# A hybrid decoder layer on one core: the third group's chain moved beside the next head pair's first inverse

## What is computed

```python
def step(S, inp):
    r_t, w_t, k_t, v_t, kk_t, b_t = inp
    sa = jnp.einsum('bhvk,bhk->bhv', S, -kk_t)
    S = S * w_t[:, :, None, :] + sa[..., None] * b_t[:, :, None, :] + v_t[..., None] * k_t[:, :, None, :]
    y = jnp.einsum('bhvk,bhk->bhv', S, r_t)
    return S, y
_, ys = lax.scan(step, S0, (tm(r), tm(decay), tm(k), tm(v), tm(kk), tm(b)))
# per head: y = (y - mean) * rsqrt(var + GN_EPS) * gn_w + gn_b, then
bonus = jnp.sum(r * k * r_k, axis=-1, keepdims=True) * v
y = y + bonus
```

## Time and profile before

| | us |
|---|---|
| median of 3 runs (1468.05 to 1469.26) | 1469.11 |
| profiled execution, device time | 1467.6 |
| its span | 1465.8 |
| TensorE matmul busy (PE) | 1352.2 |
| VectorE busy (DVE) | 722.3 |
| ScalarE busy (ACT) | 663.2 |
| GpSimd busy (POOL) | 475.7 |
| chain that ended last: TensorE 73%, VectorE 18%, ScalarE 5% | |

### The profile page before, as it was taken

One profiled execution on the slowest core, in us unless ns is written; L12 is line 12 of the kernel. 1 busy time (PEld: TensorE's weight loads), 2 busy tenths in 40 slices (PEclk: granted clock), 3 DMA queues, 4 the chain that ended last, 5 costly groups with the idle time before them and its releaser, 6 DMA issues.

```text
span 1465.8 us, 23803 instructions
## 1 busy us (share of the span) xinstructions
PE 1352.2 (92%) x9393; PEld 1141.8 (78%) x9393; DVE 722.3 (49%) x1562; ACT 663.2 (45%) x1518; POOL 475.7 (32%) x362
## 2 busy tenths in 40 slices
PE   4998989999899898998999998999999999989997
PEld 3987778777787777877768786888888888668885
DVE  5236574675755767557665543444434444540013
ACT  4334545555455454554545463444444434432221
POOL 2341222322322222232222232343433343334443
PEclk9999999999999999999999999999999999999998
DMA  5231111111111111111111121222222222225433
GB/s 200 75 88 44 44 46 52 48 41 52 46 44 53 44 44 53 44 47 44 50 44 46 56 74 51 79 73 73 73 80 70 75 73 72 72 64 171 150 97 136
DMA packets 151263, 102.23 MB, mean 70 GB/s; under 512 B 6398, under 2 KB 140640, under 8 KB 149600
## 3 DMA queue, kind: packets, MB, share of 16 engines
q1 hardware_dynamic: 151152, 100.71, 23.1%
HBM read 96.49 MB, written 4.19 MB: 69 GB/s over the span
## 4 chain that ended last, share of the span: by engine, by line
PE 73%; DVE 18%; ACT 5%; issue 2%; POOL 1%; DMA 0%; DVEq 0%; ACTq 0%; SPq 0%
PE tile L518 41%; DVE arena L1408 2%; PE tile L784 2%; DVE arena L1385 2%; PE tile L786 2%; PE tile L785 2%; PE ma L750 2%; PE ma L638 2%; DVE arena L1342 2%; PE ma L662 1%; DVE arena L1397 1%; DVE arena L1337 1%; PE mb L765 1%; PE mb L710 1%; PE mb L705 1%
## 5 line engine op out<-in xcount | busy, mean ns | idle before, releaser
L1125 POOL TENSOR_TENSOR w_lo<-w_raw,w_hi 128x512 fp32r<-128x512 f32 x324 | 426.6, 1317 | 940.8 <-ACT w_hi L854 940.6
L518 PE MATMUL tile<-hn_hi,w_hi 128*128 128x264 f32 (+1 forms) x1696 | 452.2, 329 | 0.0
L518 PE MATMUL tile<-hn_lo,w_hi 128*128 128x264 f32 (+1 forms) x1696 | 434.0, 319 | 0.0
L518 PE MATMUL tile<-hn_hi,w_lo 128*128 128x264 f32 (+1 forms) x1696 | 431.6, 318 | 0.3
L854 ACT CAST w_hi<-w_raw 128x512 fp32r<-128x512 f32 x324 | 200.5, 619 | 315.1 <-PE tile L518 205.8
L518 PEld LDWEIGHTS tile<-hn_hi,w_hi 128*128 128x128 f32 x1696 | 277.5, 190 | 32.9 <-issue 16.1
L518 PEld LDWEIGHTS tile<-hn_hi,w_lo 128*128 128x128 f32 x1696 | 275.8, 189 | 15.7 <-ACT arena L1013 1.7
L518 PEld LDWEIGHTS tile<-hn_lo,w_hi 128*128 128x128 f32 x1696 | 275.6, 189 | 13.5 <-issue 0.5
L1413 DVE TENSOR_TENSOR arena<-ma,c 128x384 f16<-128x384 f32 x120 | 66.6, 555 | 84.3 <-PE ma L638 84.1
L1010 ACT ACTIVATE arena<-ma 128x384 f16<-128x384 f32 x120 | 58.6, 488 | 46.4 <-PE ma L655 43.6
L1013 ACT ACTIVATE arena<-ma 128x384 f16<-128x384 f32 x120 | 58.2, 485 | 0.0
(11 more groups left out here) (248 smaller groups left out, 2145.4 us busy)
## 6 DMA issues: line engine op xcount, KB each, us to landing
w_raw<-w_in SPq DMA_DIRECT2D x260, 256.0 KB, 2.8
w_raw<-w_out SPq DMA_DIRECT2D x64, 256.0 KB, 3.0
big<-x SPq DMA_DIRECT2D x4, 1024.0 KB, 8.1
arena<-x SPq DMA_DIRECT2D x4, 1024.0 KB, 9.5
out<-big SPq DMA_DIRECT2D x3, 1024.0 KB, 3.9
arena<-post_norm_w SPq DMA_DIRECT2D x1, 1024.0 KB, 4.9
out<-big SPq DMA_DIRECT2D x2, 512.0 KB, 3.2
arena<-table_rope SPq DMA_DIRECT2D x2, 264.0 KB, 2.9
```

What stands on the lines that cost most here:

```text
L518: last = mm(o[:, at:at + n], w[:, slot, cols], t[:, kt, tok:tok + n], start=(kt == 0 and w is w_hi and t is hn_hi), stop=(kt == KT - 1 and ...
L1125: T(w_lo[:, slot, :], w_raw[:, slot, :], w_hi[:, slot, :].bitcast(F32), ALU.subtract).then_inc(s("lo_done"), 1)
```

## The change

- The late chain of group 2 no longer lies in the next pair's stage but beside its first inverse: `chain_at` puts a chain's step at step 4.25 + n of the inverse of group (g+1) mod 3, right behind an inverse step. In iteration 9 (attention) it stays at the start.
- For that, what the late chain still reads gets a place of its own: a second set of suv for the last three chunks (`chunk_home`), a second `w_end`, and a third `bk_tok` and `b_in`; `wu` and `au` share their columns, `tha` its place with `lv`.
- The first inverse starts at place 11.5 instead of 12.5, an inverse takes 17.2 slots instead of 16.8. The bonus goes from place 24 to 12.8, the group norm from 10.68 to 25.2.
- `ar_pads` of groups 1 and 2 are two pieces; the last one comes at the end of the first inverse.
- The level masks are made one per level, each behind the sum before it, and the two k masks at levels 2 and 3, where both stood together at the start.

No arithmetic changes. The core of the diff:

```diff
-        INV_AT, INV_SPAN, INV_STEPS = 12.5, 16.8, 15.19
-        CHAIN_LAG, CHAIN_SPAN, CHAIN_STEPS = 0.18, 16, 11
-        LATE_AT, LATE_SPAN = 4.97, 7.71
-        GN_AT = 10.68
-        BONUS_AT = 24
-        GATE_AT = 24
+        INV_AT, INV_SPAN, INV_STEPS = 11.5, 17.2, 15.19
+        CHAIN_FROM = 4.25
+        LATE_AT, LATE_STEP = 0.85, 0.7
+        GN_AT = 25.2
+        BONUS_AT, BONUS_DVE = 12.8, 15.3
+        GATE_AT = 37.5
-        REST_DVE = (8.58, 9.5, 13.5)
+        REST_DVE = (8.58, 9.3, 10, 10.6)
-        LEVEL_1, LEVEL_2 = 1.6, 3.92
+        LEVEL_1 = 1.6
+        MASK_AFTER = (2, 3)
...
-        def chain_at(g, step, late, work="rwkv"):
-            if late:
-                return (LATE_AT if work == "rwkv" else 0.5) + LATE_SPAN * step / CHAIN_STEPS
-            return INV_AT + INV_SPAN * (g + 1) + CHAIN_LAG + CHAIN_SPAN * step / CHAIN_STEPS
+        def chain_at(g, step, late, work):
+            if late and work == "attn":
+                return LATE_AT + LATE_STEP * step
+            return inv_at((g + 1) % NG, CHAIN_FROM + step)
+
+        def chunk_home(i, ch, late=0):
+
+            return ch + GC * ((i - late) % 2) if ch >= NC - GC else ch
...
-                    yield chain_at(g, 0.5 + 3 * c, late, work)
+                    yield chain_at(g, 3 * c, late, work)
...
-                yield chain_at(NG - 1, 3 * GC - 1, True)
-                if gn:
-                    dve.wait_ge(s("u_done"), n * NC - NC)
-                ar_pads(rest)
                 yield REST_DVE[2]
                 STT(rkp[:, 0:TP], xr[:], column(par, PC["r_k"], i - 1), kp, ALU.mult,
                     ALU.mult).then_inc(s("rkp_made"), 1)
-                yield BONUS_AT + 0.5
+                yield REST_DVE[3]
+                ar_pads(middle)
+                yield BONUS_DVE
                 dve.wait_ge(s("bonus_done"), n)
                 TT(mixed(i - 1), mb[:, 0:SEQ], xv[:, CH:TP], ALU.mult).then_inc(s("bonus_taken"), 1)
-                yield chain_at(0, 0, 0) - 0.5
+                yield inv_at(0, 12.8)
+                if gn:
+                    dve.wait_ge(s("u_done"), (n - 1) * NC)
+                ar_pads(last_)
...
                 for l in range(1, LEVELS):
                     yield inv_at(g, 1.7 + 2 * l)
                     dve.wait_ge(s("zz_done"), n * 5 + (l - 5))
                     TT(g3(z16), g3(ma[:, 0:W]), every(ident16), ALU.add).then_inc(s("zz_taken"), 1)
-                    if l == 1:
-                        yield inv_at(g, LEVEL_2)
-                        for l2 in range(2, LEVELS):
-                            level(l2, l4[:, l2 - 1])
-                        TT(g3(ab_lo), ab32, g3(ab_hi), ALU.subtract).then_inc(s("levels_made"), 1)
+                    yield inv_at(g, 1.8 + 2 * l)
+                    if l + 1 < LEVELS:
+                        level(l + 1, l4[:, l]).then_inc(s("level_made"), 1)
+                    else:
+                        TT(g3(ab_lo), ab32, g3(ab_hi), ALU.subtract).then_inc(s("lo_kept"), 1)
+                    if l in MASK_AFTER:
+                        yield inv_at(g, 2.6 + 2 * l)
+                        dve.wait_ge(s("kb_copied"), n)
+                        mask_k(MASK_AFTER.index(l))
```

More of the change, by code:

```diff
@@ L161, in hybrid_layer @@
         t512b = tanh_g[:]
-        ARENA = 16184
+        ARENA = 16192
         arena = sb("arena", [P, ARENA])
@@ L179, in hybrid_layer @@
         gn_pow = carve("rwkv", "gn_pow", 8)
-        wu = carve("rwkv", "wu", P)
-        au = carve("rwkv", "au", P)
+        wu = au = carve("rwkv", "wu_au", P)
         ew = carve("rwkv", "ew", NC * (CH + 1))
         ew3 = ew.rearrange("p (c t) -> p c t", c=NC)
-        w_end = carve("rwkv", "w_end", NC)
+        w_ends = [carve("rwkv", f"w_end{b}", NC) for b in range(2)]
         kk_small = carve("rwkv", "kk_small", 2 * TG)
@@ L192, in hybrid_layer, with several @@
         bk = carve("rwkv", "bk", NC * P).rearrange("p (c t) -> p c t", c=NC)
[L193 to L200, removed]
+        suv = carve("rwkv", "suv", (NC + GC) * P).rearrange("p (c t) -> p c t", c=NC + GC)
+        def several(count, name, n, dt=F32):
+            return [carve("rwkv", f"{name}{b}", n, dt) for b in range(count)]
+        bk_tok = several(NG, "bk_tok", GC * P)
+        t_t = several(2, "t_t", GC * P)
+        b_in = several(NG, "b_in", GC * 2 * P)
         b_in3 = [v.rearrange("p (c t) -> p c t", c=GC) for v in b_in]
@@ L208, in hybrid_layer @@
         emi = carve("rwkv", "emi", TPX)
-        tha = carve("rwkv", "tha", TP)
         kk = carve("rwkv", "kk", TP)
         kp = carve("rwkv", "kp", TP)
+        shared = taken["rwkv"]
+        tha = carve("rwkv", "tha", TP)
+        taken["rwkv"] = shared
+        lv = carve("rwkv", "lv", (LEVELS - 1) * GC * P, F16)
         ab_hi = carve("rwkv", "ab_hi", GC * P, F16)
         ab_lo = carve("rwkv", "ab_lo", GC * P, F16)
-        lv = carve("rwkv", "lv", (LEVELS - 1) * GC * P, F16)
         x16 = carve("rwkv", "x16", GC * P, F16)
@@ L1018, in chain_act @@
                     ch = g * GC + c
-                    yield chain_at(g, 0.8 + 3 * c, late, work)
+                    home = suv[:, chunk_home(i, ch, late), :]
+                    yield chain_at(g, 3 * c + 0.3, late, work)
                     if 0 < ch < SC:
@@ L1022, in chain_act @@
                         if ch == 1:
-                            act.wait_ge(s("ends_made"), i)
+                            act.wait_ge(s("ends_made"), i - late)
                         for h, rows in enumerate(halves):
-                            last = A(state0[rows, :], suv[rows, ch, rows], ACT.Copy, scale=w_end[rows, ch:ch + 1])
+                            last = A(state0[rows, :], home[rows, rows], ACT.Copy, scale=w_end_of(i, late)[rows, ch:ch + 1])
                         last.then_inc(s("s_scaled"), 1)
-                    yield chain_at(g, 1.8 + 3 * c, late, work)
+                    yield chain_at(g, 3 * c + 1.3, late, work)
                     if 0 < ch < SC:
@@ L1030, in chain_act @@
                     act.wait_ge(s("u_done"), chunks_so_far(i, ch, late))
-                    A(suv[bottom, ch, bottom], mb[bottom, bottom], ACT.Copy).then_inc(s("u_lower_taken"), 1)
-                yield chain_at(g, 9, late, work)
+                    A(home[bottom, bottom], mb[bottom, bottom], ACT.Copy).then_inc(s("u_lower_taken"), 1)
+                yield chain_at(g, 8.4, late, work)
                 act.wait_ge(s("y_done"), n)
@@ L1399, in inv_dve, with mask_k @@
                 yield inv_at(g, LEVEL_1)
-                level(1, l4[:, 0]).then_inc(s("level_1_made"), 1)
-                yield inv_at(g, 2)
-                dve.wait_ge(s("kb_copied"), n)
+                level(1, l4[:, 0]).then_inc(s("level_made"), 1)
                 cs = slice(g * GC, (g + 1) * GC)
-                for h, rows in enumerate(halves):
+                def mask_k(h):
                     other = halves[1 - h]
```

88 lines of the change are left out of this document (47 added, 41 removed).

## The result

| | before | changed |
|---|---|---|
| median | 1468.88 us | 1524.57 us |
| lowest to highest, 4 runs each | 1468.05 to 1469.26 | 1522.59 to 1525.44 |
| ratio, 95% interval | | 1.0375 [1.0358, 1.0393] |
| span of the profiled execution | 1465.8 | 1520.8 |
| pair to pair, pairs two to eight | 92.8 | 100.6 |

The change costs 55.7 us, 55.0 between the two profiled spans. Seven pairs that are 7.8 us longer and a first pair that is 1.7 longer make 56.3, so to about 1 us all of it lies in the head pairs. Attention and the output projection took as long as before.

A forecast was written before the change was run, and what follows sets the result against it. TensorE, busy 92% of 1465.8 us, was taken as the bound. Per iteration -1.3 + 1.1 + 1.7 + 0 = +1.5, seven +10.5, first pair -3: +7.5, so 1475, as median 1477; range 1457 to 1499.

The forecast's parts named there:

- part 1: Chain steps behind inverse steps: 67 to 53 interruptions of TensorE's projection, at 0.09 each, 1.3 us gained per iteration.
- part 2: Stretch before the first inverse without the late chain: four TensorE waits, 5.9 us together against 4.8 before, 1.1 lost per iteration.
- part 3: Group norm beside the second inverse: waits of 0.9, 0.7 and 0.3 us, 1.7 lost net per iteration.
- part 4: Waits inside the three groups, chain and inverse copies coming in couples: 6.3 us against 6.2, net 0, bounds 2 and 9.
- A: Faster: couples hidden since each chain step has a whole inverse step of time; 1446, or 1456 to 1466 us; chance 0.27.
- B: TensorE's clock falls to half rate after the waits before the first inverse in pairs two to eight: 1491 us; chance 0.10.
- C: Single level masks meeting GpSimd's subtractions make the next sum 0.3 late, 2.4 per iteration: 1494 us; chance 0.11.

The follow-up runs named there:

- e1: The changed kernel with the chain's steps half an inverse step later (4.75 in place of 4.25), between inverse steps: 1468.3 us, ratio 0.9992.
- e14: e1 with remaining pads singly between first-inverse steps, inverses opened one slot later, and TensorE's first two inner steps later: 1424.5 us, ratio 0.9699.

## Why the prediction was wrong

The direction was right, and the size was not: 1477 forecast, 1524.6 measured, outside the range. The terms per iteration, each against its measurement:

| term | forecast | measured |
|---|---|---|
| part 1, fewer interruptions | -1.3 | 53 in the trace, 67 before: -1.3 |
| part 2, stretch before the first inverse | 5.9 now, +1.1 | 2.03, 1.03, 1.54, 1.15: 5.75 now, +0.95 |
| part 3, group norm | 0.9, 0.7 and 0.3, +1.7 | 1.1 and 0.3, +1.2 |
| part 4, waits inside the groups | 0 | what is left of +7.8: **+7.0** |

**The step that failed is part 4**, "Net 0; its bounds are 2 us now (couples hidden) and 9 (each step late)". The mechanism was the right one: it named the couples, the state updates ahead of a sum and the y copies ahead of the level copies. Its size was wrong, and its upper bound was too. With before at 6.2, as I had it, the measured +7.0 means 13 us of waits in the groups. I priced a couple at what the chain's copy adds to the inverse's row (0.1, 0.3, 0.35, 0.45) against the work between the steps. By e1 against the change, couples cost 9.3 us per iteration; in the prediction's own figures, 6.3 with them and 2 if they are hidden, they cost 4.3. Three things are missing in that. The serving engine doesn't only run the chain's copy first; it waits for TensorE's second matmul of the couple while the inverse's input is there (the sum at 454.02 was 1.14 us late by both, of which the state update's own run is 0.58). Where a cast falls into a couple I allowed 0.8 per group for its own run; the one at 459.24 runs for 0.62 and before that holds ScalarE idle for 1.82, since it waits for TensorE's projection. And part of the loss is in waits too short for a row: the rows inside the groups went from 3.4 us to some 7, where the total of 13 goes by subtraction.

The first pair was to be 3 us shorter and became 1.7 longer. The same error is in it, since two of its groups have couples. In e1, which has the rest of the change without couples, it took 87.3 us against 90.6: 3.3 less, where the sum gave 3. In pairs two to eight e1 still has the waits of parts 2 and 3 at the same lengths and 8 interruptions more than before, 2.9 us in all, and takes 0.5 longer. So its groups hold 2.4 us less than before, some 4: with half a step between them the couples are nearly hidden.

**The rivals.** A (couples hidden) was the opposite of what happened, and at 0.27 it had too much weight: what spoke for it, that each chain step has a whole inverse step of time, is room on average and says nothing of the order at the moment of a couple. It is nearly true of the version with half a step between them.

B (the clock) occurred, and cost nothing that the lengths of the pairs show. Its sign was a granted clock under 1 in pairs two to eight. In the changed kernel the clock was 0.50 (the lower level, 1.2 GHz) from about 304.2 to 307.3 us in pair three, behind the wait of 2.03 for the pads, and likewise in pairs five, seven and eight (mean 0.98 each). Pairs two, four and six, with the same order, kept 1.00. What the engine did at that place in pairs three and four:

```profile
304.00:308.00 4.00, 3.98 (x18) 2.73 (x15) 3.90 (x9) 1.08 (x3) 0.00 (x0) 0.58 0.22 66
404.60:408.60 4.00, 2.97 (x21) 2.15 (x18) 3.90 (x9) 1.08 (x3) 0.00 (x0) 1.00 0.26 70
```
```profile
306.45 1.58 PE L610 MATMUL mb<-arena,c 128*128 128x512 f32 x2
...
309.85 0.33 PE L633 MATMUL ma<-c,arena 128*128 128x128 f16 x3 [1.09 <-DVE arena L1411]
```

At the lower clock TensorE was about 1 us longer at its work. It came late enough to find the bonus product made (no wait at L610, 1.03 in pair four) and waited 1.09 at L633 in place of 1.54. It then began L633 20.5 us after the start of the pair, as in pair four, and both pairs last 100.6. VectorE's row of pads was the limit there, so the slower clock filled waits. The prediction had argued that the clock would hold since no wait is over 2.0; it held in three of the seven pairs and fell in four. In e1 pairs two and five show the same (0.98, and 93.3 us like the others). In e14, where the longest wait for the pads is 1.5, all eight pairs have 1.00.

C (masks in the way) shows in TensorE's rows at one place per pair, and the kernel before paid for it as well. A wait of 1.25 us at L633 in the third group stands behind a mask held beside GpSimd's subtraction, in seven of the eight pairs. In pair four it ends at 468.08, and these are the operations:

```profile
466.53 1.40 DVE L1411 TENSOR_TENSOR arena<-arena,c 128x384 f16<-128x384 f16 x1
```
```profile
466.45 1.27 POOL L1135 TENSOR_TENSOR w_lo<-w_raw,w_hi 128x512 fp32r<-128x512 f32 x1 [5.26 <-ACT w_hi L863]
```

Before, the mask held at the same place kept the chain's copy L1432 waiting, and TensorE with it, by 1.19 in each of the eight pairs:

```profile
445.24 0.49 PE L705 MATMUL mb<-arena 128*128 128x128 f32 x2 [1.19 <-DVE arena L1432]
```

So putting nothing for such meetings was right to 0.1 us here. The wait is in e1 too, and so is no part of the 56 us that the half step gave back. The mean of the level masks is 0.409 us beside 0.407 before. In e1 the mean is 0.462, so the masks were held more often in the kernel that is 56 us faster. The Trainium skill, "SBUF — State Buffer", section "SBUF: two separate sides", has the later of two such operations blocked until the other ends. These rows agree: the subtraction ends at 467.72, and the mask ends 0.2 us later where one alone takes 0.35. The runs say that such meetings did not make the difference between the two kernels.

## What to carry to other kernels

Where two strands share serving engines that work in order, look at the written order at the moment both ask, not at the engines' average room: the strand whose result is needed next must come first, and the other should be half a step away. A chain that is set directly behind another saves interruptions of the filler (2 us per iteration here) and brings waits of 9 us. Before a stretch is rearranged, try its opening time: one slot was worth 26 to 30 us here, because several waits hung on it, and 0.7 of a slot more lost 7 again, because another engine's written place moved past a fixed one.

## What the runs showed that I had not expected

TensorE can wait for a serving engine that was idle just before: at 453.40 above, VectorE had been idle for 1.07 us, the last half of it with the inverse's input there, and TensorE then waited 0.32 for the sum. A slower clock can cost nothing where TensorE would have waited anyway: pairs with the clock at 0.50 for about 3 us are as long as pairs without. And a held operation costs little where room lies behind it: in e1 a level mask ran for 1.34 us beside GpSimd's subtraction at 431.35, where one alone takes 0.35, and of that second only 0.26 reached TensorE (L709 at 433.39, for the state update behind the mask).

```profile
431.50 1.34 DVE L1411 TENSOR_TENSOR arena<-arena,c 128x384 f16<-128x384 f16 x1
```
